# A two-block transformer kernel: the gather and routing loops written out, with another lead and other places in each engine's order

## The reference, cut to what matters

```python
q  = (xb @ w_q).reshape(T, 8, 2, 128)               # 8 heads, two halves
s  = einsum('thpd,hpkd->thpk', q, sub_keys)         # 128 scores per half
sv, si = top_k(s, 16)                               # per half
cand   = sv[:, :, 0, :, None] + sv[:, :, 1, None, :]    # 256 candidates
top_s, pos = top_k(cand, 16);  eidx = ...           # 16 experts of 16384
gate = softmax(top_s)
u   = take(expert_u, eidx);  act = gelu(einsum('thkd,td->thk', u, xb))
v   = take(expert_v, eidx);  y   = einsum('thk,thkd->td', gate * act, v)
```

## Time and profile before

| | us |
|---|---|
| Median of 3 runs | 4076.16 |
| Lowest, highest | 4074.84, 4086.30 |
| The profiled execution | 4073.35 |
| Its span in the profile | 4071.4 |

### The profile page before, as it was taken

One profiled execution on the slowest core, in us unless ns is written; L12 is line 12 of the kernel. 1 busy time (PEld: TensorE's weight loads), 2 busy tenths in 40 slices (PEclk: granted clock), 3 DMA queues, 4 the chain that ended last, 5 costly groups with the idle time before them and its releaser, 6 DMA issues.

```text
span 4071.4 us, 34938 instructions
## 1 busy us (share of the span) xinstructions
PE 2006.1 (49%) x9949; PEld 931.6 (23%) x9949; DVE 2019.2 (50%) x4967; ACT 685.6 (17%) x1897; POOL 2056.6 (51%) x2098
## 2 busy tenths in 40 slices
PE   8998963443433333333437954333333333333447
PEld 3554541111111111111213431111111111111213
DVE  1425265555555555555552255555555555555551
ACT  2112121111111111112111111111111111112112
POOL 1413136565655555555562045555555555555661
PEclk9998886666666666666568976666666666666668
DMA  5312359898988888889997268888888888889992
GB/s 199 124 52 83 134 188 340 324 342 307 345 331 331 323 329 330 327 329 361 335 341 260 83 251 333 330 330 327 333 331 328 323 330 336 325 323 357 341 362 103
DMA packets 334241, 1168.56 MB, mean 287 GB/s; under 512 B 36026, under 2 KB 39380, under 8 KB 331732
## 3 DMA queue, kind: packets, MB, share of 16 engines
q0 software_dynamic: 294912, 1073.87, 70.2%
q1 hardware_dynamic: 39124, 92.27, 6.1%
HBM read 1163.92 MB, written 2.10 MB: 286 GB/s over the span
## 4 chain that ended last, share of the span: by engine, by line
another core or an unknown queue 47%; PE 18%; ACT 10%; issue 8%; DVE 6%; POOL 3%; DMA 3%; POOLq 0%; ACTq 0%; DVEq 0%
PE banks L701 14%; ACT ring L1405 4%; PE banks L1039 4%; DVE scr L1903 2%; ACT L1397 2%; ACT L1385 2%; POOL scr L646 2%; POOL ring L652 2%; DMA ring<-in_peer_up,idx_v 1%; DMA ring<-in_expert_v,idx_v 1%; ACT scr L1385 0%; ACT hT L1223 0%; ACT ring L1375 0%; ACT scr L1397 0%
## 5 line engine op out<-in xcount | busy, mean ns | idle before, releaser
L1039 PE MATMUL banks<-ring 128*32 128x512 f32 x4096 | 874.6, 950 | 1642.2 <-ACT ring L1405 736.6
L1903 DVE CUSTOM_DVE_ANT_0 scr<-scr,banks 128x1024 f32<-128x1024 f32 x1024 | 1207.2, 1218 | 578.7 <-DMA scr<-in_expert_u,idx 271.1
L646 POOL DMA_INDIRECT scr<-in_expert_u,idx x512 | 480.9, 939 | 542.4 <-DVE idx L1882 156.0
L646 POOL DMA_INDIRECT scr<-in_peer_down,idx x512 | 480.7, 939 | 422.9 <-DVE scr L1903 155.8
L1039 PEld LDWEIGHTS banks<-ring 128*32 128x32 f32 x4096 | 177.5, 153 | 2126.3 <-issue 1983.2
L652 POOL DMA_INDIRECT ring<-in_expert_v,idx_v x512 | 480.2, 938 | 312.7 <-issue 145.7
L652 POOL DMA_INDIRECT ring<-in_peer_up,idx_v x512 | 480.6, 939 | 306.5 <-issue 150.2
L701 PE MATMUL banks<-ring,scr 128*128 128x128 f32 (+1 forms) x2112 | 287.4, 297 | 8.6 <-ACT ring L1427 5.2
L701 PEld LDWEIGHTS banks<-ring,scr 128*128 128x128 f32 x2112 | 259.7, 201 | 85.0 <-issue 81.6
L1375 ACT ACTIVATE ring<-banks 128x256 f32<-128x256 f32 x64 | 24.5, 383 | 1457.6 <-remote 1391.4
L701 PE MATMUL banks<-ring,hT 128*128 128x512 f32 x512 | 224.6, 596 | 1.8 <-DVE hT L1808 1.0
(11 more groups left out here) (211 smaller groups left out, 2067.6 us busy)
## 6 DMA issues: line engine op xcount, KB each, us to landing
ring<-in_w_mod SPq DMA_DIRECT2D x12, 2048.0 KB, 8.8
ring<-in_w_in SPq DMA_DIRECT2D x7, 2048.0 KB, 12.9
scr<-in_peer_w_q SPq DMA_DIRECT2D x1, 8192.0 KB
scr<-in_peer_down,idx POOLq DMA_INDIRECT x512
ring<-in_peer_up,idx_v POOLq DMA_INDIRECT x512
scr<-in_w_q SPq DMA_DIRECT2D x1, 8192.0 KB
scr<-in_expert_u,idx POOLq DMA_INDIRECT x512
ring<-in_expert_v,idx_v POOLq DMA_INDIRECT x512
```

The source lines that it names most:

```text
L646: nc.gpsimd.indirect_dma_start(u_rows[:, k % SLOTS, :], None, table_u, bass.IndirectOffsetOnAxis(idx[:, h % IDX_SLOTS, k:k + 1], 0)).then_ ...
L1039: last = nc.tensor.matmul(psum[2 + c][32 * g:32 * g + 32, :], spread[:, h % 2, k, :], v_rows[k % SLOTS][:, c * CW:(c + 1) * CW], start=(h ...
L1903: V.tensor_tensor_reduce(u_rows[:, k % SLOTS, :], u_rows[:, k % SLOTS, :], xn, 1.0, 0.0, ALU.mult, ALU.add, dots[:, h % 2, k:k + 1]).then_ ...
```

## The change

The loops over tiles become Python loops, so that all 32 tile-heads of a layer are written out on every engine, and every `hold` becomes a plain wait. With that, work is moved:

- POOL: the u gathers lead by `U_LEAD` = 24 instead of 16. The pair is now v(n,k), u(n+1,k+8) for k below 8, and v(n,k), u(n+2,k-8) above. The first 24 u gathers are issued ahead of the first v gather. `idx_packed` is waited for at v(n,0), `routed` at u(n,0).
- DVE: weights(n-1) stands after route(n+1), ahead of the dot products of n, instead of behind the dot products of n-1. softmax(n+1) stands after the eighth dot product. `add_output` of a tile stands after the ninth dot product of the next tile's head 1.
- PE: scores_q(n+3) stands ahead of group 0, scores_s(n+3) ahead of group 1, `move_weights` of the next head (n+1) ahead of group 3, move_idx(n+3) behind group 3. `block_rows` moves from the start of a tile's last head to the middle of the head before.
- ACT: softmax_exp(n+2) behind gelu(n). In the second layer the second pair of gate banks is copied out after the last head, from banks 6 and 7 instead of 4 and 5.

```diff
+N_HEADS = TT * PH
+U_LEAD = TOPK + SLOTS
...
-                    for h in range(PH):
-                        u_too = h < PH - 1 or more
-                        hold(pool, idx_packed, first + (h + 1))
-                        if u_too:
-                            hold(pool, routed, first + (h + 4))
-                        for k in range(TOPK):
-                            if u_too:
-                                u_gather(first + (h + 1), (h + 1) % PH, k)
-                            v_gather(first + h, h, k)
...
+                for i in range(U_LEAD):
+                    u_gather(i // TOPK, i % TOPK)
                 full(pool, *last_projection)
...
+                for i in range(N_HEADS * TOPK):
+                    v_gather(i // TOPK, i % TOPK)
+                    if i + U_LEAD < N_HEADS * TOPK:
+                        u_gather((i + U_LEAD) // TOPK, (i + U_LEAD) % TOPK)
...
+                def add_up(j):
+
+                    n, h = n0 + j, j % PH
+                    if h == 0:
+
+                        pe.wait_ge(x_added, n // PH + 1)
+                    if j + 3 < N_HEADS:
+                        scores_q(j + 3)
                     for b in range(TOPK // QUADS):
-                        if b == 2 and scores_too:
-                            scores_q(n + 3, (h + 3) % PH)
-                        if b == 3 and scores_too:
-                            scores_s(n + 3, (h + 3) % PH)
+                        if b == 1 and j + 3 < N_HEADS:
+                            scores_s(j + 3)
+                        if b == 2 and h == PH - 2 and j + 2 < N_HEADS:
+
+                            pe.wait_ge(u_used, (n + 2) * TOPK + SLOTS)
+                            block_rows()
+                        if b == 3 and j + 1 < N_HEADS:
+                            move_weights(j + 1)
...
+                    if j + 3 < N_HEADS:
+                        move_idx(j + 3)
...
+                def head(j):
+
+
+                    more = j + 1 < N_HEADS
                     if more:
-                        route(n + 1, (h + 1) % PH)
-                    if h == 0:
-                        hold(dve, xn_ready, blocks)
-                    dot_products(n, h)
+                        route(j + 1)
+                    weights(j - 1)
+                    if j % PH == 0:
+                        dve.wait_ge(xn_ready, (n0 + j) // PH + 1)
+                    dot_products(j, range(SLOTS))
                     if more:
-                        softmax(n + 1, (h + 1) % PH)
-                    weights(n, h)
+                        softmax(j + 1)
+                    dot_products(j, range(SLOTS, SLOTS + 1))
+                    if j % PH == 1 and j > PH:
+                        add_output(j // PH - 1)
+                    dot_products(j, range(SLOTS + 1, TOPK))
                     if more:
-                        pack_idx(n + 1, (h + 1) % PH)
+                        pack_idx(j + 1)
```

More of the change, by code:

```diff
@@ L276, in gates @@
         for n in range(2):
-            jobs.add(("gate", t, n), "A", (4 if t == 1 else 6) + n)
+            jobs.add(("gate", t, n), "A", 6 + n)
     def products(t):
@@ L969, in keys, with peer, scores_q @@
                     last.then_inc(bank_ready, 1)
[L971 to L974 removed]
+            def peer(layer, raw_keys, name, w, norm, beside):
+                n0 = layer * N_HEADS
+                def scores_q(j):
+                    n, h = n0 + j, j % PH
+                    if h == 0 and j > 0:
+                        pe.wait_ge(x_cur_set, n // PH + 1)
                     q = psum[4 + h % 2][:, 0:2 * P]
[L977 removed]
+                    if j >= 2:
                         pe.wait_ge(s_copied, n - 1)
@@ L993, in scores_s, with scores @@
                     last.then_inc(s_done, 1)
-                def scores(n, h, first=False):
-                    scores_q(n, h, first)
-                    scores_s(n, h)
+                def scores(j):
+                    scores_q(j)
+                    scores_s(j)
                 def block_rows():
@@ L1078, in peer @@
                 pe.wait_ge(x_cur_set, layer * TT + 1)
-                scores(layer * TT * PH, 0, first=True)
+                scores(0)
                 block_rows()
-                scores(layer * TT * PH + 1, 1, first=True)
+                scores(1)
                 project(name, 1, w, (1,))
-                move_idx(layer * TT * PH, 0)
+                move_idx(0)
                 for t in (2, 3):
@@ L1088, in peer @@
                 all_empty(pe, "nt", norm, 3, 1)
-                scores(layer * TT * PH + 2, 2)
-                move_idx(layer * TT * PH + 1, 1)
-                with pe.Fori(0, TT - 1) as b:
-                    token_block(b + layer * TT, True)
-                token_block(TT - 1 + layer * TT, False, beside)
+                scores(2)
+                move_idx(1)
+                move_weights(0)
+                move_idx(2)
+                for j in range(N_HEADS):
+                    add_up(j)
+                    if j - (TT - 1) * PH in beside:
+                        beside[j - (TT - 1) * PH]()
             w = [use_chunk("w_out", CW * n) for n in range(2)]
@@ L1444, in peer @@
                 all_empty(act, "nt", norm, 3, 1)
-                scores_out(n0 + 2, 2)
-                activations_and_weights(n0, 0, move_bank(0, False))
-                scores_out(n0 + 3, 3)
-                with act.Fori(0, TT - 1) as b:
-                    token_block(b + layer * TT, b, True)
-                token_block(TT - 1 + layer * TT, TT - 1, False, beside)
+                scores_out(2)
+                for j in range(N_HEADS):
+                    head(j)
             no_shift = lambda k: 0.0
@@ L1951, in peer @@
                 tile_out(norm, 0, gains, shifts)
-                route(n0, 0)
-                softmax(n0, 0)
+                route(0)
+                softmax(0)
                 add_projection(1, (1,))
@@ L1961, in peer @@
                 tile_out(norm, 1, gains, shifts)
-                dot_products(n0, 0, range(SLOTS // 2, SLOTS))
-                route(n0 + 1, 1)
+                dot_products(0, range(SLOTS // 2, SLOTS))
+                route(1)
                 add_projection(3)
                 tile_stats(norm, 3)
-                dot_products(n0, 0, range(SLOTS, TOPK))
-                softmax(n0 + 1, 1)
-                weights(n0, 0)
-                pack_idx(n0 + 1, 1)
-                with dve.Fori(0, TT - 1) as b:
-                    token_block(b + layer * TT, b, True)
-                token_block(TT - 1 + layer * TT, TT - 1, False, beside)
+                dot_products(0, range(SLOTS, TOPK))
+                softmax(1)
+                pack_idx(1)
+                for j in range(1, N_HEADS):
+                    head(j)
+                weights(N_HEADS - 1)
+                add_output(TT - 1)
             early = range(TT - 1)
```

210 lines of the change are left out of this document (92 added, 118 removed).

## The result

The changed kernel takes 3813.6 us (median of 4 runs, 3805.4 to 3815.3) against 4076.5 us before on the same chip: a ratio of 0.9355, 95% interval 0.9336 to 0.9375, or 263 us less. I forecast 3914, 162 less.

A forecast was written before the change was run, and what follows sets the result against it. Bound: a stream of gathers with holes, POOL pausing twice a head. 4073.35 - 184 (shorter heads, both layers) + 22 (starts and ends) = 3911, profiled 2.8 below the median, so 3914 us; range 3680 to 4040.

The forecast's parts named there:

- Pause A: POOL's 7.78 us pause ahead of u(n,8), read as waiting for DVE's first dot product; to go with the lead of 24.
- Two pauses take its place, no third: POOL pauses ahead of v(n,8) and v(n,0), 47.8 us a head; rival third pause: about 4140 us, chance 0.17.
- a sign against me: The forecast counts as wrong if pauses stand at v(n,4) or v(n,12), gaps vanish, or u(n,8) keeps its long pause.
- the rule: While gathers run back to back PE's signals are held, POOL runs out of permitted gathers, and the drain releases them.
- groups 1 and 3 end within 5.4 us of a release: PE's groups 1 and 3 run right after a release, so their signals pass and cause no further POOL pause.
- 3.8 us per pause: Cost of each of two POOL pauses per head: 39.8 + 2 x 3.8 = 47.4 us, plus 0.4 for short pauses.
- B-type pauses: POOL pauses like the one ahead of v(n,0), 4.16 us long, costing 3.8 or 3.9, waiting for PE's late signal.
- Plain waits at zero: Written-out loops and plain waits change nothing: POOL's gap of 0.30 us holds in both forms; zero.
- Start of a layer, 8.7 us lost: u(1,8) still needs dot product (1,0), so seven gathers are behind at POOL's start: 7 x 1.24 = 8.7 us.
- End, 2.3 us lost each: 24 v gathers follow u(31,15) instead of 16: 57 us instead of 44.4, but u(31,15) comes 9.9 earlier; 2.3 lost.
- ACT's copy of q 12 us late: Expected sign in the trace: ACT's copy of q still 12 us or more behind its product on PE.
- The rival "signals pass": Group 0's signal mostly slips through, one pause a head: 3686 us, chance 0.12; no pause, 40.7 a head: 3488, 0.03.

The follow-up runs named there:

- old_places_16: Changed kernel with lead 16 and weights, move_weights, move_idx, add_output at the old places: 3609.3 us on the third chip (1.0194 to before), 3610.3 on the fifth (1.0188).
- no_pe_return: Changed kernel, but add_up multiplies a fixed tile of X and v gathers don't wait for PE's groups; output not the reference's: 4391.4 us, 1.0791 to before.
- hold_back: Changed kernel with the increment of an unused semaphore put back behind each of POOL's two waits per pair: 3872.0 us, 0.9523 to before.
- third to fifth chips: Later measurements on three different chips, where the kernel before takes 3542, 3540 and 3541 us instead of 4076 and 4071 on the first and second.
- after_again: The unaltered changed kernel run again beside the kernel before, on the fourth chip: 3521.8 us against 3540.2, ratio 0.9947.
- fourth chip: The chip where the changed kernel was run again beside the kernel before: 3521.8 us against 3540.2, ratio 0.9947.

## Why the prediction was right, and where it was not

- **Pause A goes.** Right: 24 u gathers of lead gave DVE the slack. But I took pause A for DVE's own time. `old_places_16` shows no such pause at a lead of 16 where signals are not late; the better reading, argued above and not shown, is late signals that reach POOL through DVE.
- **Two pauses take its place, no third.** Nearly right in number: 135 pauses stand ahead of v(n,8), v(n,4) and v(n,0) in both layers, about 2.2 a head. Wrong in one place: the second stands mostly ahead of v(n,4), which I had named as a sign against me. That the pauses gained at v(n,4) (8 before, 47 now) were roughly made up by those that went at v(n,0) (56 before, 28 now) was luck; the rule did not give it. The step that failed is that groups 1 and 3 end within 5.4 us of a release and so pass: group 3 ran at 1237.36, 25 us after the last stop (ahead of v(13,8), until 1212.81), and its signal was held from 1241.0 to 1247.08; group 2's passed earlier, singly, with the DMA engines full. The row behind that step said less than I took from it: before, group 3 ended at 1241.2 and v(13,4) ran without a pause at 1246.58, so its signal passed somewhere in 5.4 us, not at once. Nor does a signal need a stop, as `no_pe_return` shows. Signals are held less strictly than my rule says.
- **3.8 us per pause.** This is the term that was mis-sized. Head: 39.8 + 8.0 forecast, 39.8 + 6.8 measured; of the 6.8 the three places above make 5.7 (2.2 pauses of 2.6 us net of the gap), the short pauses 0.8 where I had 0.4. Over 60 heads 258 us were saved instead of 184, 74 of the 101 us by which I missed. B-type pauses measured 4.05 before (57 of them, each behind 15 to 19 gathers without a stop); after, those behind 15 to 19 are 3.2 (46), those behind 5 to 9 are 2.4 (59), those behind 20 or more 2.5 (28). So the distance between stops is part of it at most: pauses at the same distance are shorter too, and those at the longest distance are not long. The cause is open.
- **Plain waits at zero.** Wrong: `hold_back` puts POOL's increments at about 55 us. It is part of the shorter pauses, not on top of them, and more than half of the 101 us.
- **Start of a layer, 8.7 us lost.** Next to nothing was lost: u(1,8) came at 594.09, 8.5 us earlier than in the earlier trace rows, which makes up for the seven gathers. I kept DVE's old time for the dot product (1,0), though weights(0) had stood ahead of it and waited 18.7 us for the gelu; now only pack_idx does, for 7.1 us. DVE before, then after:

```profile
591.77 0.23 DVE L1908 TENSOR_TENSOR ring<-scr,ring 128x64 f32<-128x64 f32 x1 [18.72 <-ACT scr L1397]
```

```profile
584.24 0.17 DVE L1887 CAST idx_v<-banks 128x16 uint32<-128x16 f32 x1 [7.12 <-PE banks L1000]
...
592.46 0.22 DVE L1899 TENSOR_TENSOR ring<-scr,ring 128x64 f32<-128x64 f32 x1
```

- **End, 2.3 us lost each.** From u(31,15) to the end of the last group it took 52.4 us (2007.7 to 2060.1) against 44.4 in the earlier trace rows, and 58.7 against 48.4 in the second layer: 8.0 and 10.3 longer where I had 12.2, and u(31,15) is 9.9 us earlier in the order. Start and end together came to nothing instead of 22 us; with the 74 above that is the miss but for 5 us.
- **ACT's copy of q 12 us late.** Wrong for q (median 4.7 us now, since scores_q ends just ahead of a pause), right for the weights (median 15.7).
- **The rival "signals pass"** is what the third to fifth chips do: 41.7 us a head (the first layer of `after_again`) where I had 40.7. I had given it 0.15 as something the change might bring; it came with the chip, and there the kernel before has nearly all of it already.
- **The two rules of the Trainium skill.** "Perfetto Trace Analysis", section "Tensor Engine Instruction (MATMUL, LD_WEIGHTS)", lets PE's update leave with the last write: the fourth chip agrees (0.04 us above), the first two do not (15.9 and 35 us). "DMA: Bandwidth & Descriptors", section "Specifications", puts a core at about 358 GB/s; its section "Measured (HBM→SBUF, 128 partitions, SWDGE, issued from GpSimd)" says that this is the share of each core when both of a pair stream, and that a core alone has more. The fourth chip moved 404 GB/s over 407 us, which fits a core alone; as a limit on this kernel 358 was the wrong figure.

## What to carry to other kernels

Ask of each "remote" wait how long ago the work behind it ended. If the answer is microseconds while the DMA engines are full, ask what else waits for such signals before taking a pause away: `no_pe_return` took away the pauses for PE, and one of 16.6 us a head came elsewhere. Before trusting a gain of some per cent that rests on such lateness, time both kernels on another chip. And when a stream's lead is lengthened, move ahead with it every transfer that the engine now running earlier waits for.

## What the runs showed of the hardware

Two kinds of behaviour were met. On the first two of the five chips (which may be one, see above), what PE has finished reaches ACT and POOL up to 39 us late while gathers run back to back at 408 to 411 GB/s. For the copy of q the median over 64 heads is 17 us in the kernel before, 4.7 in the changed one and 32 in `no_pe_return`. In the kernel before it runs mostly 3.0 to 3.3 us after POOL's last gather; in `no_pe_return` 0.5 to 5.6 us after it in 36 heads, and without a stop in 20. On the other three it arrives within about 0.1 us at the same rate. The kernel before takes 15% longer on the first kind, the changed one 8%. No numbered chip was met in more than one session, so whether the chip or the session makes the difference is not shown; what makes it, and which single updates slip through, stays open.

The DMA engines take time to fill again behind a pause: in the changed kernel they moved 408 GB/s from 1236 to 1246, then 115 in the 2 us behind 1247 and 321 in the 7 us behind 1249. This costs POOL nothing by itself, since its pitch stays 1.24 us and the pauses alone account for the time of a head.
